# A mixture layer's gather by pairs from one f32 copy, an eleventh weight place, and a folded pool scale

## The reference

```python
y = einsum('bsgc,gcd->bsgd', pooled, w) + b      # pooling mixer, four groups of 256 channels
return y.reshape(B, S, D) * scale
# mixture layer: each token goes to its 2 best experts of one group
h = silu(x_e @ w_gate[e]) * (x_e @ w_up[e])      # w_gate, w_up: 1024 x 512
y_e = h @ w_down[e]                              # w_down: 512 x 1024, weighted by the gate
```

## Time and profile before

| | us |
|---|---|
| median of 3 runs (lowest, highest) | 1861.36 (1857.62, 1862.13) |
| profiled execution, its own time | 1861.17 |
| its span, first to last instruction | 1859.4 |
| PE busy / weight loads | 1695.0 / 1106.6 |
| DVE / ACT / POOL busy | 854.7 / 492.6 / 46.5 |
| DMA: 542.33 MB, mean over the span | 292 GB/s |

### The profile page before, as it was taken

How to read it: one execution, slowest core, us unless ns; L and a number is a source line. 1 busy time by engine, 2 the same in 40 slices (tenths; PEclk the granted TensorE clock), 3 DMA queues, 4 the chain that set the end, 5 groups by cost and what they waited for, 6 DMA issues and landing times.

```text
span 1859.4 us, 22242 instructions
## 1 busy us (share of the span) xinstructions
PE 1695.0 (91%) x9060; PEld 1106.6 (60%) x9060; DVE 854.7 (46%) x1422; ACT 492.6 (26%) x758; POOL 46.5 (3%) x39
## 2 busy tenths in 40 slices
PE   6988999899989999699999989879889999898896
PEld 5867999897778999644443434336664444343343
DVE  3567777674657777523332213232462333232222
ACT  4445444433445444310000000012331100000001
POOL 0100000000000000300000000000020000000000
PEclk9999999999999999889999999999889999999999
DMA  9424666564544556469999999995257999999995
GB/s 373 159 68 136 203 203 194 163 202 159 187 136 159 190 171 247 183 282 421 424 426 424 426 425 426 425 420 210 105 207 296 423 425 425 425 426 425 425 425 214
DMA packets 114549, 542.33 MB, mean 292 GB/s; under 512 B 5400, under 2 KB 51616, under 8 KB 88992
## 3 DMA queue, kind: packets, MB, share of 16 engines
q1 hardware_dynamic: 113600, 536.90, 73.2%
q10 hardware_dynamic: 864, 4.24, 0.6%
HBM read 540.07 MB, written 1.05 MB: 291 GB/s over the span
## 4 chain that ended last, share of the span: by engine, by line
PE 70%; DMA 20%; DVE 5%; ACT 2%; issue 1%; POOL 1%; SPq 0%; DVEq 0%; ACTq 0%
PE PS L1841 13%; PE PS L630 11%; DMA ring<-w_up 11%; PE PS L631 11%; PE PS L632 11%; PE PS L1864 8%; DMA work<-w_up 8%; PE PS L498 2%; PE PS L1791 2%; PE PS L1792 2%; PE PS L1819 1%; PE PS L1820 1%; DMA ring<-even_w_in 1%; PE PS L1850 1%; DVE e_w_lo L663 1%
## 5 line engine op out<-in xcount | busy, mean ns | idle before, releaser
L1841 PE MATMUL PS<-ring,work 128*64 128x512 f32 x1280 | 286.8, 602 | 28.5 <-DMA ring<-w_up 23.7
L1841 PEld LDWEIGHTS PS<-ring,work 128*64 128x64 f32 x1280 | 98.4, 139 | 212.4 <-issue 212.1
L1917 DVE SCALAR_TENSOR_TENSOR work<-PS,small,work 128x512 f32<-128x512 f32 x32 | 24.0, 751 | 411.4 <-PE PS L1841 411.4
L1864 PE MATMUL PS<-ring,work 128*64 128x512 f32 x640 | 143.4, 601 | 1.6 <-ACT work L1882 1.6
L1841 PE MATMUL PS<-work 128*64 128x512 f32 x528 | 131.3, 607 | 12.7 <-DMA work<-w_up 10.2
L1895 DVE TENSOR_TENSOR y_lo<-PS,y_hi 128x512 fp32r<-128x512 f32 x64 | 44.3, 692 | 166.7 <-ACT y_hi L1888 166.7
L1882 ACT ACTIVATE work<-PS 128x512 f32<-128x512 f32 x32 | 19.1, 598 | 346.2 <-PE PS L1850 346.2
L1096 DVE TENSOR_TENSOR r_w_lo<-ring,r_w_hi 128x1024 fp32r<-128x1024 f32 x64 | 78.2, 1224 | 65.9 <-ACT r_w_hi L1089 64.7
L630 PE MATMUL PS<-f_x_hi,f_w_gate_hi 128*128 128x256 f32 x352 | 100.0, 284 | 5.4 <-DVE work L1031 3.5
L1888 ACT ACTIVATE y_hi<-PS 128x512 fp32r<-128x512 f32 x64 | 38.2, 597 | 248.3 <-PE PS L1864 248.3
L1089 ACT ACTIVATE r_w_hi<-ring 128x1024 fp32r<-128x1024 f32 x64 | 68.0, 1064 | 120.6 <-PE PS L632 120.6
(11 more groups left out here) (325 smaller groups left out, 3625.1 us busy)
## 6 DMA issues: line engine op xcount, KB each, us to landing
ring<-w_gate SPq DMA_DIRECT2D x40, 2048.0 KB, 34.3
ring<-w_up SPq DMA_DIRECT2D x40, 2048.0 KB, 32.4
ring<-w_down SPq DMA_DIRECT2D x36, 2048.0 KB, 30.8
ring<-ffn_w_up SPq DMA_DIRECT2D x22, 2048.0 KB, 8.7
work<-w_gate SPq DMA_DIRECT2D x12, 2048.0 KB, 28.4
work<-w_down SPq DMA_DIRECT2D x12, 2048.0 KB, 33.0
work<-w_up SPq DMA_DIRECT2D x12, 2048.0 KB, 35.0
ring<-ffn_w_down SPq DMA_DIRECT2D x22, 1024.0 KB, 6.1
```

Source lines behind the costliest of these rows:

```text
L1841: last = nc.tensor.matmul(PS[CAP * e:CAP * (e + 1), what, :], xg[:, c, at:at + CAP], chunk_of(w[e], c), start=(c == 0), stop=(c == DC - 1))
L1864: last = nc.tensor.matmul(PS[CAP * e:CAP * (e + 1), 2 + n, :], e_hT[:, c, CAP * e:CAP * (e + 1)], part_of(w[e], c)[n], start=(c == 0), sto ...
```

## The change

1. *Gather.* Only one f32 copy of the normalised rows remains (`hs`, made by ACT); `raw_pool`, `hs_hi` and `hs_lo` are gone, and POOL only computes the root. Each pair is gathered by itself, with 16 f32 products of 128 columns, between the up product and the transposes of the pair before it. `sel` has 128 columns and is made for each pair.
2. *Places.* The memory so freed makes a fifth extra, and the wheel turns over eleven places.
3. *Halves.* The first two units that reuse ring slots are loaded by halves, the first halves as soon as half of the first gate product is done (`half_read`). The last four units of a layer (`last_four`: up, up, down, down) are loaded by halves too, the first halves of both experts ahead, and PE starts on a first half.
4. *Combination.* `y_hi` and `y_lo` hold 512 columns, not 1,024; the two halves of a combination stand apart, the second between the two halves of the down product.
5. *Pool.* The scale is multiplied into the pool weights on DVE, and the four results are added to x straight from PSUM.
6. *Queues.* The band and row loads move from ACT's queue to SP's. On SP, the sixth unit of layer 0 moves behind three fills of extras and the new one, and in the MLA part the early fills move behind `wq_up`.

```diff
@@
-        xg = area(0, DC, 2 * P)
-        sel = placed("sel", [P, NT, 2 * P], work_at + 4 * 2048, F32R)
-        hs_hi = placed("hs_hi", [P, NT, DC, P], work_at + 4 * 2560, F32R)
-        hs_lo = placed("hs_lo", [P, NT, DC, P], hs_at, F32R)
+        xg = area(0, DC, P)
+        sel = area(1024, NT, P)
...
-                 (xnT.rearrange("p c s -> p (c s)"), area(MOE_END, 3 * BANK), area(BEYOND + UNIT, BANK))]
+                 (xnT.rearrange("p c s -> p (c s)"), area(MOE_END, 3 * BANK), area(BEYOND + UNIT, BANK)),
+                 (area(MOE_END - UNIT, UNIT),)]
...
         def pool_dve(dve, link):
 
-            dve.wait_ge(E("rows_in"), 16)
             link(nc.vector.tensor_tensor(pl_bs, R("pool_b"), R("pool_scale"), ALU.mult))
...
+                    nc.vector.tensor_tensor(v, v, bank(4 + 2 * t + n), ALU.add).then_inc(E("pool_add"), 1)
+
+        def pool_scale_dve(dve):
+
             dve.wait_ge(E("rows_in"), 16)
+            dve.wait_ge(loaded[POOL_UNIT % SLOTS], 16 * (POOL_UNIT // SLOTS + 1))
+            w = view(ring[:, POOL_UNIT % SLOTS, 0:2 * D], 4, 2, 256)
+            for c in range(2):
+                nc.vector.tensor_tensor(w[:, :, c, :], w[:, :, c, :], view(R("pool_scale"), 4, 256), ALU.mult).then_inc(E("pl_w"), 1)
...
-                nc.scalar.activation(hs_hi[:, t, :, :], x[:, t, :].rearrange("q (p c) -> q c p", c=DC), ACT.Copy,
-                                     scale=rstd[:, t:t + 1]).then_inc(E("ro_hi"), 1)
-
-        def raw_pool(pool, k, l):
...
+                nc.scalar.activation(hs[:, t, :], x[:, t, :], ACT.Copy, scale=rstd[:, t:t + 1]).then_inc(E("n_hs"), 1)
...
+        def gather_pe(q):
+
+            for b in range(2):
+                for c in range(4):
+                    for t in range(NT):
+                        last = nc.tensor.matmul(bank(GATHER[b])[:, c * P:(c + 1) * P], hs[:, t, 4 * b + c:D:DC], sel[:, t, :],
+                                                start=(t == 0), stop=(t == NT - 1))
+                last.then_inc(q["xg_ps"], 1)
...
-            if j == 1 and not final:
-                gather_pe(pe, q, g)
+            if not final:
+                q.wait(pe, "sel", s + 1)
+                gather_pe(q)
             q.wait(pe, "h", s + 1)
+            if behind(s):
+                q.wait(pe, "add", 4 * s - 4)
...
             if behind(s):
-                combine_pe(pe, q, s - 1)
+                combine_pe(pe, q, s - 1, 0)
...
-                    if n == 1:
-                        q.wait(pe, "add", 4 * s)
+                    if n and halves[0] == 0 and behind(s):
+                        combine_pe(pe, q, s - 1, 1)
...
+        def last_four(sp, units, l, first):
+
+            at = MOE_UNITS - 4
+            ups = [(units.slot(k), expert_source(l, N_EXP - 2, 2 + k)) for k in range(2)]
+            downs = [(extra[k][0], expert_source(l, N_EXP - 2, 4 + k)) for k in range(2)]
+            sp.wait_ge(used, first + at + 1 - WHEEL + 1)
+            for dst, src in ups:
+                sp.dma_start(dst[:, 0:HALF], src[:, 0:HALF]).then_inc(E("half_in"), 16)
+            for dst, src in ups:
+                sp.dma_start(dst[:, HALF:], src[:, HALF:]).then_inc(loaded[units.n % SLOTS], 16)
+                units.n += 1
...
             if l == 0:
-                units.load(units.slot(), source(SLOTS - 1))
+                sp.wait_ge(E("ffn_d"), 1 + 2 * (N_SLABS - 1))
+                sp.dma_start(pl_band.rearrange("p a b -> p (a b)"), band_in).then_inc(E("table_in"), 16)
+                sp.wait_ge(E("ffn_u_ps"), 8 * N_SLABS)
+                sp.dma_start(late[:, 0:2 * D], rows[:, 0:2 * D]).then_inc(E("rows_in"), 16)
+                sp.wait_ge(E("ffn_ps"), 4 * NT)
+                fill(4, 0, SLOTS + 4)
             sp.wait_ge(*((E("at_o_ps"), 16) if l else (E("n_tr"), 4 * 4 + 4)))
-            for k, i in ((1, 0), (3, 1), (2, 1)):
+            for k, i in ((1, 0), (3, 1), (2, 1)) + ((4, 0),) * l:
                 fill(k, i, SLOTS + k)
-            if l == 1:
-                units.load(units.slot(), source(SLOTS - 1))
+            units.load(units.slot(), source(SLOTS - 1))
...
+            sp.wait_ge(E("half_read"), l + 1)
+            for k in range(2):
+                sp.dma_start(units.slot(k)[:, 0:HALF], source(WHEEL + k)[:, 0:HALF]).then_inc(E("half_in"), 16)
```

More of the change, by code:

```diff
@@ L1836, in pair_pe @@
                 for c in range(DC):
-                    if what == 0 and gathered and c % 2 == 0:
-                        gathered(c)
+                    if what == 0 and c % 4 == 0:
+                        if gathered:
+                            gathered(c // 4)
+                        else:
+                            q.wait(pe, "xg", 2 * s + c // 4 - 1)
+                    if what and final and c == 4:
+                        units.wait(-2)
+                        units.wait(-1)
                     for e in range(2):
-                        at = P * j + CAP * e
-                        last = nc.tensor.matmul(PS[CAP * e:CAP * (e + 1), what, :], xg[:, c, at:at + CAP], chunk_of(w[e], c),
+                        last = nc.tensor.matmul(PS[CAP * e:CAP * (e + 1), what, :], xg[:, c, CAP * e:CAP * (e + 1)], chunk_of(w[e], c),
                                                 start=(c == 0), stop=(c == DC - 1))
+                    if gathered and what == 0 and c == 3:
+                        last.then_inc(E("half_read"), 1)
                 last.then_inc(q["gu_ps"], 1)
@@ L1982, in moe_load @@
                         fill(i % WHEEL - SLOTS, piece, i)
-            for dst, src in ends:
-                sp.dma_start(dst, src).then_inc(E("last_half"), 16)
-            units.more += EX * ROUND_OF_EXTRA
+            last_four(sp, units, l, first)
+            units.more += ELSEWHERE
             more = more_steps(l)
@@ L2029, in moe_pe @@
             for s in range(N_PAIRS):
-                pair_pe(pe, q, s // 2, s % 2, lambda k: unit(6 * s + k), *((None, None) if s else (spread_rows, gathered)),
-                        final=(l + 1) * (s == N_PAIRS - 1))
-            combine_pe(pe, q, N_PAIRS - 1)
+                pair_pe(pe, q, s, lambda k: unit(6 * s + k), *((None, None) if s else (spread_rows, gathered)),
+                        final=(l + 1) * (s == N_PAIRS - 1), units=units)
+            for n in range(2):
+                combine_pe(pe, q, N_PAIRS - 1, n, final=True)
             more = more_steps(l)
@@ L2090, in moe_dve @@
             route_rest_dve(dve, link, l)
-            for f in range(2):
-                q.first(dve, "xg_ps", f + 1)
-                fill_dve(q, l, FIRST_FILLS[f], f)
+            for b in range(2):
+                q.first(dve, "xg_ps", b + 1)
+                fill_dve(q, l, b)
             link(v.tensor_scalar(slot_id, C("slot"), 0.0, None, ALU.add))
@@ L2219, in _ @@
             ret_pool(pool)
-            for k in range(3, 5):
+            for k in range(3, 7):
                 norm_pool(pool, k)
-            raw_pool(pool, 5, 0)
-            norm_pool(pool, 6)
             mla_pool(pool)
-            raw_pool(pool, 7, 1)
-            norm_pool(pool, 8)
+            for k in range(7, 9):
+                norm_pool(pool, k)
         @block.vector
```

348 lines of the change are left out of this document (161 added, 187 removed).

## The result

The changed kernel takes **1946.13 us** (median of 4 runs, 1943.42 to 1946.86) against 1859.70 (4 runs, 1857.62 to 1862.13) before: a ratio of 1.0459, 95% interval [1.0442, 1.0476]. It is 86 us slower. The forecast was 1826.8 us.

A forecast was written before the change was run, and what follows sets the result against it. The mixture layers were taken as bound by weight transfers, their start set by pair 0's down release. Layers -16.1 and -11.6, tails -4.0 and -2.7, sum -34.4 from 1861.2: 1826.8 us, range 1816 to 1838.

The forecast's parts named there:

- step 4: Each pair's f32 gather: 16 products at 0.24 us, 3.8 us in all; first gather -2.5 us, narrower selection about -0.5.
- Step 7: Every pair gathers: 26.9 us on PE against 29.6 of DMA; 11 us of slack, 0.75 per pair.
- G: Start of a layer's first expert matmul; forecast 787.9 in layer 0, near 1372 in layer 1 on the new time line.
- Rival D: Gather at half clock: 7.6 us, a pair of 30.7, +92, 1918 us; decides from a 5.7 us gather; chance 0.03.
- Rival C: PE shares the bound: a 4.5 us gather uses up the slack; at 5.0 us +15, 1842 us; chance 0.07.
- rival E: Pooled transposes ahead of G run at full clock, saving 2.5 us; with the whole tail gain 1823 us; no separate chance.
- 1, loads: Band and row loads leave ACT's queue, so norm 4's fourth square comes earlier: -2.6 us in layer 0.
- 2, pool scale: Pool scale multiplied into the weights on DVE, shorter adds after the pool matmuls: -1.0 us in layer 0.
- 3, POOL: Without POOL's high and low copies, DVE's operations from router logits to selection speed up: -5.5 us in each layer.
- 5, releases: Pair 0's down release moves from G + 27.4 to G + 28.5 and decides among three starts; early halves worth 0.
- 6, eleventh place: One more unit of stock, full in both layers before use: 4.93 us less per layer.
- 8, tail: From last up weights to down product, with loads by halves: -4.0 us in layer 0, -2.7 in layer 1.

The follow-up runs named there:

- experiment 1: Changed kernel, but ACT writes the normalised rows in chunk order, so the gather's stationary columns lie side by side; 1826.8 us, ratio 0.9843; repeated later, 1831.9 us.
- experiments 1 to 4: After experiment 1: changed kernel with gather column steps 1, 2, 4, 8 (1883.6 us); steps 3, 8, 15, 5 (1921.4); first steps in f32r, high part alone (1823.8).
- experiments 1 and 5: The second: experiment 1's kernel with four of each gather's sixteen contiguous products made twice; 1852.7 us, ratio 0.9967.
- experiment 8: Experiment 1's kernel with band and row loads back on ACT's queue, the row load behind the wait for FFN output; 1834.8 us, ratio 0.9886.
- experiment 7: Experiment 1's kernel with POOL's product and subtraction per token tile put back, into a spare area; 1842.8 us, ratio 0.9925.
- experiment 9: Experiment 1's kernel with pair 1's gather behind pair 0's down product, not ahead of its transposes; 1831.9 us, ratio 0.9868.
- experiment 12: Experiment 1's kernel with the eleventh place first filled behind pair 0's down release, in both layers; 1835.3 us, ratio 0.9877.
- experiment 10: Experiment 1's kernel with the eleventh place first filled behind pair 0's gate release, in both layers; 1827.5 us, ratio 0.9848.

## Why the prediction was wrong

**The step that failed is 4**, the price of the new gather's products: "Such a one takes 0.22 us in the pooled transposes; strided stationary columns have a row at 0.131 each for one load, and two loads make 0.26. I take 0.24." The first row is a contiguous load and right for one: experiment 1 has 0.223. The second was to stand for the step. But it is a row of transposes. Their loads in the kernel before, with the same 8 elements between columns:

```profile
L1572 PEld LDWEIGHTS PS<-tables,x_res x32: 186/190/206, 771.7 to 1374.9; 128*128 128x128 f32 x32
```

They stay at 190 ns, while a product's load goes from 192 to 335 (experiments 1 to 4). The upper bound was therefore no bound. The gather was 7.83 us. By the Trainium skill ("TensorE: Matmul & The Clock Gate", LDWEIGHTS) a load's time goes by its number of columns, and that section has no term for the step; all loads compared here have 128, and they take 192 to 335 ns, so for a product's load the measurements decide against it as far as the step goes.

**Step 7 fell with it.** "PE 26.9, DMA 29.6, slack 0.75 per pair" became 31.28 against 29.6. From experiment 1 to the changed kernel, PE's last gate product of layer 0 goes from G + 414.4 to G + 470.1, 55.7 us; the first gather has 4.1 more. Twice their sum is 119.6, and the medians lie 119.3 apart (117 from 1829). Step 7 was too generous even with a gather of 3.77: the pair is 27.20 and not 26.9, which takes 3 us of the slack, and PE starts on the first half of the last up weights about 2 us ahead of the landing that the slack was counted to. It is not 11 us but 5.5 and 5.3, what PE waits in experiment 1, and a gather of 4.67 has used it up.

**Rival D had the place, the arithmetic and nearly the price** (a gather of 7.6 us, a pair of 30.7, 1918 us, deciding from 5.7), but not the cause: it wants the half clock, and the changed kernel's granted clock is 1.00 (2.4 GHz) where the gathers take 7.83. Rival C had the right mechanism, with a deciding point of 4.5 us where experiments 1 and 5 give about 4.1. The Trainium skill's four passes ("FP8 and Floating Point Precision", TensorE Precision Notes) make an estimate of 3.4 us a gather, near the contiguous gather's 3.77; of the step they say nothing.

**The other terms held**, as experiment 1 shows, where only step 4's fault is mended: G at 784.4 and in its repetition 782.9 (forecast 787.9), in layer 1 at 1371.3 and 1366.5 (1372). Part of this is not the change's: FFN 1's last addition itself starts at 746.97 and 748.12, at 750.01 before. From there to G it is 37.4 and 34.8 us, forecast 37.9. The 2.6 between the two are rival E's: the pooled transposes run at half clock in experiment 1 and at full clock in its repetition, the same kernel.
- *1, loads:* -2.6; the fourth square 2.5 us later with them back (experiment 8), and the pool product 2.5 us earlier behind the last addition in experiment 1 than in the kernel before (12.4 and 14.9).
- *2, pool scale:* not tried alone. Its cost and gain are inside G's.
- *3, POOL:* -5.5; measured 5.0 from addition to selection (experiment 7). What else that experiment's total holds stays open.
- *5, releases:* down release at 812.92 in experiment 1, G + 28.5 as forecast; in the changed kernel at 821.69, G + 32.6. That of the three starts of pair 0 the last decides is right, but a fourth, pair 1's gate release, is close behind (experiment 9).
- *6, eleventh place:* -4.93; measured 4.8 to 4.9 of transfer, all of it felt by PE where the clock is alike (experiment 12). Last up weights in at G + 423.2 and + 423.3, forecast G + 423.6.
- *8, tail:* down product at G + 430.7 and + 430.5, forecast G + 430.5.

That experiment 1's first median is the forecast to the tenth is chance, since its repetition gave 5 us more. That both lie within the forecast's range follows from the terms above.

## What to carry to other kernels

A bound of a price must come from a row of the same instruction in the same mode: a transpose's load says nothing of a product's, though the tile, the step and the type agree. Before a gather or any product takes its stationary operand from every n-th element, pay for the order once where the tile is written (here ACT's copy went from 2.17 to 4.23 us for both tiles, off the critical path) and not at each of 512 loads per layer. And where two resources have nearly the same time per turn (here 27 and 29.6 us), give every price on the one below the bound its own worst case times the number of turns: the first third of a microsecond in a gather is hidden, and 3.57 us in each of 32 gathers cost 100 us.

## What the runs showed of the hardware

- A product's weight load of 128 columns takes 192, 199, 261, 329, 314, 334 and 326 ns with a step of 1, 2, 3, 4, 5, 8 and 15 f32 elements, and in f32r within 2 ns of that at 1, 2, 4 and 8. Transposes load in 190 ns with a step of 8 (kernel before) and in 209 with a step of 4 (L1843 of the changed kernel). Why they differ stays open, as does what a step does to the moving operand; neither was tried.
- The slow load hardly depends on the clock. The changed kernel's first gather takes 7.91 us, though the granted clock is 0.50 in 784 to 787, and the later ones, at 1.00, take 7.83. A contiguous gather goes from 3.84 to 5.3 or 5.4 when as long a stretch at 0.50 falls in it (782 to 784 and some on either side in experiment 10):

```profile
780.00:785.00 5.00, 4.43 (x36) 3.99 (x38) 3.17 (x13) 0.00 (x0) 0.00 (x0) 1.00 0.08 31
```

```profile
780.00:785.00 5.00, 3.64 (x19) 3.43 (x19) 2.81 (x15) 0.00 (x0) 0.00 (x0) 0.66 0.35 144
```

  The first is experiment 1 (first gather 3.84 us), the second experiment 10 (5.34). Up to there the two differ in one early load alone, and experiment 9, which doesn't differ at all, has 5.40 as well: 1.5 us there come and go between executions.
- More comes and goes between the layers. From the end of layer 0's last down product to G of layer 1, the profiled executions of experiment 1 and its repetition, the same kernel, take 147.8 and 143.1 us, at a granted clock of 0.88 and 0.92. So where a few us matter, a reading counted from G says more than a total.
